# Expert activations stored by blocks of four tiles, gates loaded by two groups, and the first group's loads moved into the stage before

## The reference, cut to what matters

```python
act = gelu(einsum('cd,chkd->chk', x, u_experts[idx]))   # 8 heads x 16 chosen experts per token
out = einsum('chk,chkd->cd', gate * act, v_experts[idx])
```

## Time and profile before

| | |
|---|---|
| median of 3 runs | 2024.35 us (2022.98 to 2035.23) |
| the profiled execution | 2025.17 us, span 2023.3 us |
| PE busy | 1868.2 us, 92% of the span |
| DVE, ACT, POOL busy | 1497.6, 720.6, 780.8 us |
| DMA moved | 526.33 MB in 325795 packets, mean 260 GB/s |
| granted TensorE clock | 0.965 of full speed |
| expert stage | about 785 to 1469 us |
| last stage | 1477 us to the end; PE from 1487.2 to 2002 us |

### The profile page before, as it was taken

The page is one execution under the profiler, slowest core; times in us unless marked ns, Lnnn a source line. Parts: engine busy times, 40 slices in busy tenths (PEclk is TensorE's granted clock), DMA queues, the critical chain, the costliest instruction groups (busy, mean ns, idle before and its releaser), DMA issues. The chain is left out here.

```text
span 2023.3 us, 28278 instructions
## 1 busy us (share of the span) xinstructions
PE 1868.2 (92%) x10096; PEld 1632.8 (81%) x10096; DVE 1497.6 (74%) x2260; ACT 720.6 (36%) x969; POOL 780.8 (39%) x487
## 2 busy tenths in 40 slices
PE   4999979999898799989999998999969999999997
PEld 4788757777777688989999988898858888888886
DVE  6566377774446488999895688888858887888887
ACT  3222234444323222323333354555533333333331
POOL 0000096000041001568787787888622332322320
PEclk7999989999999899999999999999979999999999
DMA  8799288878582431669999989999999999999991
GB/s 294 239 334 319 93 214 225 242 215 244 170 277 42 93 77 35 157 177 268 294 268 287 270 256 311 313 316 319 331 361 381 383 384 366 363 355 354 362 352 64
DMA packets 325795, 526.33 MB, mean 260 GB/s; under 512 B 20266, under 2 KB 243291, under 8 KB 321116
## 3 DMA queue, kind: packets, MB, share of 16 engines
q1 hardware_dynamic: 288860, 391.23, 64.2%
q0 software_dynamic: 36864, 134.23, 19.4%
HBM read 438.88 MB, written 85.99 MB: 259 GB/s over the span
## 5 line engine op out<-in xcount | busy, mean ns | idle before, releaser
L123 PE MATMUL u_s<-h_hi,u_hi 128*128 128x384 f32 x1024 | 358.1, 350 | 46.3 <-POOL u_lo L1857 41.6
L124 PE MATMUL u_s<-h_lo,u_hi 128*128 128x384 f32 x1024 | 348.8, 341 | 0.0
L125 PE MATMUL u_s<-h_hi,u_lo 128*128 128x384 f32 x1024 | 348.8, 341 | 0.0
L123 PE MATMUL v_o<-v_v_hi,v_w_hi 128*128 128x512 f32 x768 | 299.9, 391 | 18.7 <-DVE v_w_lo L2080 18.0
L124 PE MATMUL v_o<-v_v_lo,v_w_hi 128*128 128x512 f32 x768 | 299.7, 390 | 0.0
L125 PE MATMUL v_o<-v_v_hi,v_w_lo 128*128 128x512 f32 x768 | 299.5, 390 | 0.0
L2019 ACT ACTIVATE v_v_hi<-v_raw 128x1024 fp32r<-128x1024 f32 x128 | 127.7, 1053 | 340.0 <-PE v_o L125 268.3
L123 PEld LDWEIGHTS u_s<-h_hi,u_hi 128*128 128x128 f32 x1024 | 197.0, 192 | 59.6 <-POOL u_lo L1857 39.4
L1857 POOL TENSOR_TENSOR u_lo<-u_ut,u_hi 128x1024 fp32r<-128x1024 f32 x79 | 198.4, 2511 | 89.2 <-ACT u_hi L1635 89.1
L2046 DVE TENSOR_TENSOR v_v_lo<-v_raw,v_v_hi 128x1024 fp32r<-128x1024 f32 x128 | 149.4, 1221 | 87.8 <-ACT v_v_hi L2019 87.5
L124 PEld LDWEIGHTS u_s<-h_lo,u_hi 128*128 128x128 f32 x1024 | 197.2, 193 | 0.0
(11 more groups left out here) (313 smaller groups left out, 3803.0 us busy)
## 6 DMA issues: line engine op xcount, KB each, us to landing
v_raw<-in_v_experts_dram SPq DMA_DIRECT2D x128, 512.0 KB
u_raw<-in_u_experts_dram SPq DMA_DIRECT2D x160, 256.0 KB
expert_acts<-u_ao SPq DMA_DIRECT2D x64, 384.0 KB
u_raw<-turned_experts SPq DMA_DIRECT2D x96, 256.0 KB
expert_gates<-u_gs SPq DMA_DIRECT2D x12, 2048.0 KB, 12.0
v_gt<-expert_gates SPq DMA_DIRECT2D x32, 768.0 KB
w_in_raw<-in_w_in_dram SPq DMA_DIRECT2D x17, 1024.0 KB, 11.7
proj_ada<-in_w_ada_dram SPq DMA_DIRECT2D x8, 2048.0 KB, 13.1
```

The lines of the kernel that those rows point to most:

```text
L123: nc.tensor.matmul(out, w[0], x[0], start=first, stop=False)
L124: nc.tensor.matmul(out, w[0], x[1], start=False, stop=False)
L125: return nc.tensor.matmul(out, w[1], x[0], start=False, stop=last)
```

## The change

It does four things.

- `expert_acts` is laid out by groups of four tiles, `[32, 128, 4, 384]`. A store of two tiles writes runs of 3072 bytes in place of 1536, and a load of a group reads runs of 6144 bytes.
- From group 2 on, gates are loaded for two groups in one DMA (1.5 MB in runs of 1024 bytes, 15 DMAs), into buffers twice as large. Group 1's gates are loaded alone, as the first DMA of the last stage. A pair of groups is loaded when the weighting of the group before (`w_ok`) has been done, ahead of the activations of the next even group.
- Group 0's gates are loaded in the last turn of the expert stage, without the last chunk, which is still in the buffer `gs` and is read from there; DVE's multiplication for each of the four tiles becomes two, of 352 and 32 numbers. SP waits for the stores of the chunks before it issues that load. The first two value tiles no longer wait for the low part of the last tile, but for the one two tiles earlier.
- `g_fin` and `gate2` are loaded after the last group's values, and SP's hardware loop over the groups is written out.

The constant `LATE` is 0, so the functions around it leave the number and the order of gathers and adds as they were; `ht` is not used. What moves on the queues of SP and DVE:

The diff, cut to its core:

```diff
 def expert_groups(a, acts):
-    return a["v_experts"][0].rearrange("(g x p) d -> g p x d", x=GT, p=P), acts.rearrange("(g x) p t -> g p x t", x=GT)
+    return a["v_experts"][0].rearrange("(g x p) d -> g p x d", x=GT, p=P), acts
...
+def gates_of(gates, n):
+    return gates.rearrange("c j (g x) t -> g j c (x t)", x=n)
...
-            def store(n, j):
-                sp.wait_ge(sem["act_ok"], 2 * n + 2)
-                sp.dma_start(au[n], ao[j][:, :, :]).then_inc(sem[f"a_out{j}"], 16)
+            def store(g, j):
+                sp.wait_ge(sem["act_ok"], GT * g + 2 * j + 2)
+                to = acts[g, :, 2 * j:2 * j + 2, :] if isinstance(g, int) else acts[bass.ds(g, 1), :, 2 * j:2 * j + 2, :].rearrange("o p x t -> (o p) x t")
+                sp.dma_start(to, ao[j][:, :, :]).then_inc(sem[f"a_out{j}"], 16)
...
                     if last and x == UNROLL // 2 - 2:
                         vv, av = expert_groups(a, acts)
                         sp.dma_start(at0[:, :, :], av[0]).then_inc(w_in0, 16)
-                        sp.wait_ge(sem["lo_ok"], TILES)
+                        for y in range(2):
+                            sp.wait_ge(sem[f"g_out{y}"], 16 * (TURNS - y))
+                        sp.dma_start(gt0[:, 0:CHUNKS - 1, :], gates_of(gates, GT)[0][:, 0:CHUNKS - 1, :]).then_inc(w_in0, 16)
                         for y in range(GT):
+                            if y % 2 == 0:
+                                sp.wait_ge(sem["lo_ok"], TILES - 2 + y)
                             sp.dma_start(v[:, y, :], vv[0][:, y, :]).then_inc(v_in[y], 16)
...
-            def weights(g, j):
-                sp.dma_start(at[j][:, :, :], av[g]).then_inc(sem[f"w_in{j}"], 16)
-                sp.dma_start(gt[j][:, :, :], gv[g]).then_inc(sem[f"w_in{j}"], 16)
-
-            sp.dma_start(gt[0][:, :, :], gv[0]).then_inc(sem["w_in0"], 16)
-            weights(1, 1)
+            def weights(g):
+                sp.dma_start(at[g % 2][:, :, :], av[g]).then_inc(sem[f"w_in{g % 2}"], 16)
+
+            def gate_pair(i):
+                sp.dma_start(gt[i % 2][:, :, :, :].rearrange("p c y n -> p c (y n)"), gv[i]).then_inc(sem[f"gt_in{i % 2}"], 16)
+
+            sp.dma_start(gt[0][:, :, 1, :], gv1).then_inc(sem["gt_in0"], 16)
+            weights(1)
             values(1)
+            gate_pair(1)
+            for g in range(2, NG):
+                if g % 2 == 0 and g + 2 < NG:
+                    sp.wait_ge(sem["w_ok"], g - 1)
+                    gate_pair(g // 2 + 1)
+                sp.wait_ge(sem["wlo_ok"], g - 1)
+                weights(g)
+                values(g)
+            sp.wait_ge(sem["w_ok"], NG - 3)
             sp.dma_start(g_fin[:, :], a["g_final"].rearrange("(o d) -> o d", o=1).to_broadcast([P, D])).then_inc(sem["gf_in"], 16)
             sp.dma_start(gate2[:, :], gate2_row.to_broadcast([P, D])).then_inc(sem["gf_in"], 16)
-            with sp.Fori(1, NG // 2) as i:
-                for j in range(2):
-                    sp.wait_ge(sem["wlo_ok"], 2 * i + j - 1)
-                    weights(2 * i + j, j)
-                    values(2 * i + j)
...
             def weigh(g):
                 j = g % 2
-                dve.wait_ge(sem[f"w_in{j}"], 32 * (g // 2) + 32)
+                i = g // 2
+                dve.wait_ge(sem[f"w_in{j}"], 16 * i + 16 * (2 - j))
+                dve.wait_ge(sem[f"gt_in{i % 2}"], 16 * (i // 2) + 16)
                 x = at[j][:, :, :].rearrange("p x (c t) -> p x c t", t=CH)
-                nc.vector.tensor_tensor(x, x, gt[j][:, :, :].rearrange("p c (x t) -> p x c t", t=CH), ALU.mult).then_inc(sem["w_ok"], 1)
+                nc.vector.tensor_tensor(x, x, gt[i % 2][:, :, j, :].rearrange("p c (x t) -> p x c t", t=CH), ALU.mult).then_inc(sem["w_ok"], 1)
...
                 if x < GT:
-                    o = at[0][:, x, :].rearrange("p (c t) -> p c t", t=CH)
-                    nc.vector.tensor_tensor(o, o, gt[0][:, :, x * CH:(x + 1) * CH], ALU.mult).then_inc(sem["w0_ok"], 1)
+                    o = at[0][:, x, 0:NT - CH].rearrange("p (c t) -> p c t", t=CH)
+                    nc.vector.tensor_tensor(o, o, gt0[:, 0:CHUNKS - 1, x * CH:(x + 1) * CH], ALU.mult)
+                    o = at[0][:, x, NT - CH:]
+                    nc.vector.tensor_tensor(o, o, gs[1][:, x, :], ALU.mult).then_inc(sem["w0_ok"], 1)
...
-        acts = nc.dram_tensor("expert_acts", [NE // P, P, NT], F32, kind="Internal").ap()
+        acts = nc.dram_tensor("expert_acts", [NE // P // GT, P, GT, NT], F32, kind="Internal").ap()
```

More of the change, by code:

```diff
@@ L1502 @@
 NSLOT = PH * TOPK
+LATE = 0
+SOON = NSLOT - LATE
+LATE_BY = 16
 def dots_by(t):
@@ L1509, in dots_by, with phase_experts @@
         return EARLY_DOTS * max(0, t + 1 - DOTS_FROM) // plain
-    return EARLY_DOTS + (NSLOT - EARLY_DOTS) * (t + 1 - PLAIN) // GATED
+    return EARLY_DOTS + (SOON - EARLY_DOTS) * (t + 1 - PLAIN) // GATED
 def rows_by(t):
-    return 0 if t < KNOWN_AT else min(NSLOT, dots_by(t + 1 if t + 1 < PLAIN else t) + RING)
-def phase_experts(nc, a, keep, scores, top, topi, acts, gates, turned, raw, u_in, v, at0, v_in, w_in0, rows, few):
+    return 0 if t < KNOWN_AT else min(SOON, dots_by(t + 1 if t + 1 < PLAIN else t) + RING)
+def gates_of(gates, n):
+    return gates.rearrange("c j (g x) t -> g j c (x t)", x=n)
+def phase_experts(nc, a, keep, scores, top, topi, acts, gates, turned, raw, u_in, v, at0, gt0, gs, ht, v_in, w_in0, rows, few):
     with ExitStack() as stack:
@@ L1533, in phase_experts @@
         gs_at = k.at
-        gs = [k.sb(f"gs{j}", [P, P, CH]) for j in range(2)]
-        end = k.at
+        end = gs_at + 32 * KB
         k.at = gs_at
@@ L1598, in _ @@
                     load(2 * i + j + 2, j)
-                    store(2 * i + j, j)
+                    store(i, j)
             for j in range(2):
@@ L1602, in _ @@
                 load_turned(j, j)
-                store(PLAIN // 2 - 2 + j, j)
+                store(PLAIN // GT - 1, j)
             def turn(i, last=False):
@@ L1612, in turn @@
                         gates_out(2 * i + x // 2, x // 2)
-                    store(n, x % 2)
+                    store(PLAIN // GT + i * (UNROLL // GT) + x // 2, x % 2)
                     if last and x == UNROLL // 2 - 2:
@@ L1930, with late_by, late_slot, phase_combine @@
 VRING = 8
+def late_by(g):
+    return LATE * min(g, LATE_BY) // LATE_BY
 def adds_by(g):
-    return NSLOT * g // (NE // P // GT - 1)
-def phase_combine(nc, a, keep, acts, gates, gate2_row, x2, out, v, at0, v_in, w_in0, rows, few):
+    return (NSLOT + LATE) * g // (NE // P // GT - 1) - late_by(g)
+def late_slot(n):
+    return SOON + n
+def phase_combine(nc, a, keep, acts, gates, gate2_row, x2, out, v, at0, gt0, gs, ht, v_in, w_in0, rows, few):
     with ExitStack() as stack:
@@ L1943, in phase_combine @@
         v_lo = [k.sb("v_lo0", [P, GT, D], F32R)]
-        at1 = k.sb("at1", [P, GT, NT])
-        at = [at0, at1]
-        gt = [k.sb(f"gt{j}", [P, CHUNKS, GT * CH]) for j in range(2)]
-        ssq, fin, root = (k.sb(n, [P, TT]) for n in ("ssq", "fin", "root"))
[L1948 to L1953, removed]
+        gt = [k.sb(f"gt{j}", [P, CHUNKS, 2, GT * CH]) for j in range(2)]
+        assert k.at <= AT0_AT
+        kl = Kit(nc, stack, "v", LOW + 32 * KB)
+        gate2, g_fin = kl.sb("gate2", [P, D]), kl.sb("g_fin", [P, D])
+        k.at = Y_AT + 48 * KB
+        w_hi = [k.sb(f"w_hi{j}", [P, GT, NT], F32R) for j in (1, 0)][::-1]
+        w_lo = [k.sb(f"w_lo{j}", [P, GT, NT], F32R) for j in range(2)]
+        at = [at0, k.sb("at1", [P, GT, NT])]
+        ssq, fin, root = (k.sb(n, [P, TT]) for n in ("ssq", "fin", "root"))
         assert k.at <= X2_AT
@@ L1973, in phase_combine @@
         vv, av = expert_groups(a, acts)
-        gv = gates.rearrange("c j (g x) t -> g j c (x t)", x=GT)
+        gv, gv1 = gates_of(gates, 2 * GT), gates_of(gates, GT)[1]
         NG = NE // P // GT
@@ L2005, in _ @@
         def _(pool):
-            for n in range(NSLOT):
-                if n >= VRING:
-                    pool.wait_ge(sem["add_ok"], n - VRING + 1)
-                gather_rows(nc, ring[n % VRING], a["v_experts"], few["idx"], n).then_inc(row_in[n % VRING], 16)
+            at_row = 0
+            for g in range(1, NG):
+                for n in range(adds_by(g - 1), adds_by(g)):
+                    if at_row >= VRING:
+                        pool.wait_ge(sem["add_ok"], at_row - VRING + 1)
+                    gather_rows(nc, ring[at_row % VRING], a["v_experts"], few["idx"], n).then_inc(row_in[at_row % VRING], 16)
+                    at_row += 1
         @block.scalar
@@ L2108, in _ @@
             dve.wait_ge(sem["gf_in"], 32)
[L2109 removed]
+            dve.wait_ge(sem["add_ok"], NSLOT + LATE)
             total(0, p_a[:, :])
```

33 lines of the change are left out of this document (17 added, 16 removed).

## The result

| | before | changed |
|---|---|---|
| median | 2027.63 us (4 runs, 2022.98 to 2035.23) | 2055.32 us (4 runs, 2049.21 to 2059.0) |
| profiled execution | 2025.17 us, span 2023.3 | 2056.18 us, span 2054.4 |
| last store issued, next stage's first issue | 1469.74, 1477.15 | 1479.48, 1487.40 |
| last stage, first issue to the end | 546.15 us | 567.0 us |
| PE's waits in the last stage after its first matmul | 0.7 us | 13.6 us |

The change makes the kernel slower: ratio 1.0132, 95% interval 1.0108 to 1.0156, so 22 to 32 us. The forecast was no change (2024.5, range 2011 to 2035). The spans of the two profiled executions differ by 31.1 us: 9.7 in all that precedes the last store, 0.5 at the switch (7.92 against 7.41), 20.9 in the last stage. (Before, PE's last matmul ends at 2013 us, not at 2002 as the table of the kernel before has it.)

A forecast was written before the change was run, and what follows sets the result against it. The prediction took PE to bound the last stage and DMA the gated part. Terms -2.6 + 2.5 + 0.2 = +0.1 us on 2025.17 gave 2025.3, as median 2024.5 us (no change), range 2011 to 2035.

The forecast's parts named there:

- What bounds the kernel: Whole kernel: PE bounds the last stage (busy 93.00 of 93 us), DMA the gated part (share 1.00), not the plain part.
- Point 4, later groups: Last stage: a pair's burst of 6.6 MB takes 17.3 us, with 9 us left after the next splits; cost nothing.
- rival E: Last stage: every second group late if loads run under 243 GB/s; 2 us in 14 groups, 2053 us; chance 0.03.
- Point 4, groups 1 and 2: Last stage's start: group 1's 0.7 us wait goes, group 2 ready 0.5 us later; +0.2 us together with the extra weightings.
- Point 2, early gates: Switch to the last stage: group 0's gates in the full queue delay the last store; +2.5 us, ends +1.7 and +6.3.
- Point 2, fewer packets at the switch: Switch: 768 packets fewer from group 0's activations and three stores; 0.7 us less, already within the +2.5 us.
- Point 3, two weightings for one: Start of the last stage, DVE: four more instructions delay PE's first matmul by 0.5 us, ends 0 and 1.1.
- Point 1, larger stores: Gated part of the expert stage: 3072 packets fewer save 2.6 us, ends 0 and 13.8; plain part counted at nothing.
- rival C: Whole kernel: only bytes count, so larger stores gain nothing; 2028.0 us, as median 2027.2; chance 0.14.

The follow-up runs named there:

- e1: The changed kernel with each pair of gates issued on SP behind the even group's four values, not ahead of its activations; ratio to before 1.0031.
- e6: The changed kernel with an odd group's weighting on DVE ahead of the even group's adds, SP's order untouched; ratio to before 1.0063.
- e4: The changed kernel with group 0's gates loaded at the last stage's start, one weighting instruction per tile, first four values together; ratio to before 1.0149.
- e8: The changed kernel with pairs of gates behind the values and group 0's gates loaded at the last stage's start; ratio to before 1.0030.
- e2: The kernel before with the new layout of the activations alone (stores in 3072-byte pieces, loads in 6144); ratio to before 1.0008.
- e3: The kernel before with SP's loop written out and only the added wait for the odd group's weighting, gates single; ratio to before 1.0022.
- e10: The kernel before with pairs of gates issued behind the even group's values, old layout, group 0's gates as before; ratio to before 1.0010.
- e7: The kernel before, old layout and single gates, with the changed kernel's switch (early gates of group 0, two weighting instructions per tile); ratio to before 0.9996.
- e5: The changed kernel with an even group's activations issued on SP ahead of the added wait and the pair of gates, values behind; ratio to before 1.0054.
- e9: The changed kernel with single gates in their old place on SP, new layout and early gates of group 0 kept; ratio to before 1.0025.
- e11: e9 with each store of two tiles issued as two DMAs of one tile, in pieces of 1536 bytes; ratio to before 1.0033.

## Why the prediction was wrong

- **What bounds the kernel** was read right for the kernel before, and the conclusion drawn from it was wrong: that PE never waits in the last stage says nothing of how the loads have to be ordered to keep it so.
- **Point 4, later groups: this is the step that failed.** I wrote "Nothing", after laying one burst of 6.6 MB at 381 GB/s (17.3 us) against the time to the next splits and 9 us of slack. The runs show a loop in its place, whose length PE's pace does not cover: 33.9 us for two groups against 32.7, and with e1 or e6 the stage is back at 545.7 or 550.7 us from 567.0. Two things were missing. First, slack that is read from one passage is used up when every loop is 1.2 us longer than PE's two groups: behind its wait at group 2 PE ran eight groups without one, and then waited at eight of the ten even groups from 10 to 28. How much of the loss hangs on the late group 2 was not tested. Second, the loop had to be added up: burst, last low value, low weights, adds, weighting. From the changed trace: pair to last low value 23.4 us (1743.38 to 1766.80), to the adds 3.1, adds 6.8, weighting 1.8, together 35.0 us. The burst alone, which I had at 17.3, ends when ACT gets the last value at 1765.71, after 22.3 us:

```profile
1743.38:1765.70 22.32, 22.32 (x100) 18.46 (x99) 16.69 (x13) 4.67 (x4) 4.53 (x5) 1.00 1.01 379
```

The rate was right, 379 GB/s; the bytes were not, since 8.5 MB pass in that time and not 6.6. What else was under way then: the four gathers issued at 1737.79 to 1741.96, just before the pair (2.1 MB, in part served by then), and the odd group's activations, issued at 1749.59 (0.8 MB). The trace doesn't say how much of either is in the 8.5.
- **The rival E** (0.03) named the right groups, every second one: PE's nine waits all lie at even groups. Its mechanism was another, a rate under 243 GB/s; the rate was 344 over 1577 to 1950. That its 2053 us stands near the measured 2055.3 is luck.
- **Point 4, groups 1 and 2.** Group 1's wait of 0.72 us is gone, as said. Group 2 was to wait about 0.4 us, at most 4.1; PE waits 2.80 us. The 0.5 MB more were counted, but not that the activations stand behind the second pair on SP, whose wait for group 1's weighting and slow issue held them until 1507.80.
- **Not in the sum: slower matmuls after pauses.** PE's busy time in the stage grew by 7.7 us, 5.0 of it in three stretches with slices at a granted clock of 0.50.
- **Point 2, early gates, +2.5 us.** Right with large pieces, as far as one execution of each tells: 2.5 us (7.92 against e4's 5.43) and 2.8 (e1 against e8). With the old layout 0.8. e4 and e8 also undo the earlier value loads, so the term holds both.
- **Point 2, fewer packets at the switch, -0.7 us.** Mis-sized: without early gates it takes 5.2 to 5.4 us with the new layout (e2, e4, e8) and 7.4 to 9.0 with the old (before, e3, e10), some 3 us.
- **Point 3, two weightings for one, +0.5 us.** From the stage's first issue to PE's first matmul 10.27 us with it (changed, e1, e7) and 10.06 without (before, e2, e8): +0.2.
- **Point 1, larger stores, -2.6 us.** Wrong in sign, as far as single executions tell: the last store goes out at 1478.7 on average of seven executions with large pieces (e5 left out, 1475.1 to 1482.3) and at 1472.4 of six with small ones (1469.7 to 1476.8), 6 us later. From the first load of a turned tile to the last store it is 331.6 us (329.9 to 333.0) against 326.5 (323.8 to 326.1, and e3 at 332.3), so 5 us of it lie in the gated part. I took a DMA-bound stage to gain what DMA saves. The waits say that it hangs on whichever transfer comes last, and the larger pieces moved that from the turned tiles to the gathered rows: the rows come by the queue of POOL, the stores and the turned tiles by that of SP, and both queues run on the 16 engines. That a queue with larger pieces takes more of the engines is the explanation that fits; the waits show its effect and not its working. The Trainium skill, page "DMA: Bandwidth & Descriptors", section Queues, rings and completion order, says that an engine goes round between its queues by packets; by that rule larger packets on one queue would delay the other, and e9 against e11 agrees (60.1 us of waiting for gathered rows against 34.4).
- **The rival C**, larger pieces gain nothing, holds for the time (e2, e10), though not because they change nothing.

So of some 27 us the order on SP makes about 21; e1, which mends it alone, leaves 1.0031. Those last 6 us are not taken apart by runs: the gated part is some 5 us longer with large stores, the early gates cost 2.5 to 2.8 at the switch and the larger pieces give back some 3 there, each of them too small for the totals to show. No version here beats the kernel before: e7, at 0.9996, equals it.

## What to carry over

When a wait is put on a queue that issues in order, follow what it releases until it comes back to itself, and add up that loop against the period of the bound engine; slack read from a settled state covers a late passage, not one that comes again with every loop. A prefetch with much time to spare belongs behind the urgent loads, not ahead of them. In a stage bound by DMA, ask which of the transfers comes last, and whether a cheaper one only takes its turn.

## What the runs showed of the hardware

- In the changed kernel pauses of PE of 2.80, 3.51 and 2.52 us (ending at 1536, 1806 and 1943) were each followed by slices at a granted clock of 0.50; pauses of 1.29, 1.03 and 1.10 us (1670, 1704 and 1908) left it at 1.00. In e2 one of 2.10 us was followed by slices at 0.63 and 0.51. The three longer ones, 8.8 us of waiting, cost 5.0 us more in slower matmuls.
- DMA engines with packets under way the whole time (a share of 1.00 or more) moved 310 GB/s in the gated part and 381 in the last stage before, 379 in the burst above: the share of busy time says little of how much more they could do.
- At equal bytes the gated part took 331.6 us with stores in pieces of 3072 bytes (seven executions) and 326.5 in pieces of 1536 (six).
